# A hybrid mLSTM and Fourier mixing layer on one core: head loop rotated by four projections, value tiles finished one by one, shorter Newton chain

## The reference

```python
proj = h @ p['w_in'][l]
q, k, v, o, gt, uf, ga, gb = jnp.split(proj, SPLITS, axis=-1)
# per head and direction
s = jnp.einsum('bhtd,bhsd->bhts', qc, kc) * w
num = jnp.einsum('bhts,bhsv->bhtv', s, vc) + inter[..., None] * jnp.einsum('bhvd,bhtd->bhtv', C, qc)
den = s.sum(-1) + inter * jnp.einsum('bhd,bhtd->bht', n, qc)
h = num / jnp.maximum(jnp.abs(den), jnp.exp(-mt))[..., None]
...
hn = (hf - mu) * lax.rsqrt(var + LN_EPS) * p['mh_gain'][l].reshape(N_HEADS, DV)
y_a = (hn * og).reshape(B, S, DM).astype(h.dtype) @ p['w_branch_a'][l]
merged = jax.nn.sigmoid(ga) * y_a + jax.nn.sigmoid(gb) * y_b
return merged @ p['w_out'][l], finals
```

## Time and profile before

| | us |
|---|---|
| runs, median of 3 (lowest, highest) | 1640.36 (1639.74, 1650.82) |
| profiled execution, its own time | 1646.21 |
| its span, first to last instruction | 1644.4 |
| TensorE busy | 1518.4 (92%) |
| VectorE busy | 652.5 (40%) |
| ScalarE busy | 314.3 (19%) |
| GpSimd busy | 801.4 (49%) |

### The profile page before, as it was taken

How to read it: one execution, slowest core, us unless ns; L and a number is a source line. 1 busy time by engine, 2 the same in 40 slices (tenths; PEclk the granted TensorE clock), 3 DMA queues, 4 the chain that set the end, 5 groups by cost and what they waited for, 6 DMA issues and landing times.

```text
span 1644.4 us, 24556 instructions
## 1 busy us (share of the span) xinstructions
PE 1518.4 (92%) x9889; PEld 1476.9 (90%) x9889; DVE 652.5 (40%) x1028; ACT 314.3 (19%) x489; POOL 801.4 (49%) x365
## 2 busy tenths in 40 slices
PE   7999899999999899899886998894999999999994
PEld 7997899988989789889886998894999999999994
DVE  6422600226526525624766496457334111100114
ACT  0422211222212122122231000125211111100002
POOL 2541355652453263254147564456666666655662
PEclk9999999999999999899997999896999999999997
DMA  8220122321321221131164453310433222242221
GB/s 339 87 65 26 53 96 87 118 77 55 110 77 62 92 89 56 55 120 52 46 205 161 144 179 125 121 55 23 153 115 115 68 72 77 77 150 72 79 70 64
DMA packets 56092, 159.73 MB, mean 97 GB/s; under 512 B 5944, under 2 KB 20544, under 8 KB 54856
## 3 DMA queue, kind: packets, MB, share of 16 engines
q1 hardware_dynamic: 39464, 145.73, 25.8%
q10 hardware_dynamic: 16544, 12.82, 2.4%
HBM read 141.20 MB, written 17.33 MB: 96 GB/s over the span
## 4 chain that ended last, share of the span: by engine, by line
PE 75%; DVE 12%; issue 4%; ACT 3%; DMA 2%; POOL 2%; SPq 1%; ACTq 0%; DVEq 0%; POOLq 0%
PE psum L684 58%; PE psum L954 7%; PE psum L927 2%; PE psum L769 2%; PE psum L710 1%; PE psum L883 1%; DVE mod_sum L1419 1%; DMA mod_first<-in_wmod 1%; POOL w_hi L592 1%; PE psum L744 1%; PE psum L1015 1%; DMA raw<-in_wunits 1%; POOL r_all L656 1%; DVE h_sb L1557 1%; PE psum L843 1%
## 5 line engine op out<-in xcount | busy, mean ns | idle before, releaser
L592 POOL TENSOR_TENSOR w_hi<-raw,zero 128x1024 fp32r<-128x1024 f32 x156 | 307.1, 1969 | 652.2 <-PE psum L684 560.1
L596 POOL TENSOR_TENSOR w_lo<-raw,w_hi 128x1024 fp32r<-128x1024 f32 x164 | 413.9, 2524 | 83.2 <-ACT w_hi L1122 71.0
L684 PE MATMUL psum<-h_hi,w_hi 128*128 128x256 f32 x1600 | 373.8, 315 | 49.5 <-POOL w_lo L596 21.7
L684 PE MATMUL psum<-h_lo,w_hi 128*128 128x256 f32 x1600 | 370.9, 313 | 0.0
L684 PE MATMUL psum<-h_hi,w_lo 128*128 128x256 f32 x1600 | 369.9, 313 | 0.0
L684 PEld LDWEIGHTS psum<-h_hi,w_hi 128*128 128x128 f32 x1600 | 296.4, 193 | 53.6 <-issue 28.7
L684 PEld LDWEIGHTS psum<-h_lo,w_hi 128*128 128x128 f32 x1600 | 298.5, 192 | 0.0
L684 PEld LDWEIGHTS psum<-h_hi,w_lo 128*128 128x128 f32 x1600 | 297.4, 192 | 0.0
L1799 DVE TENSOR_TENSOR ff_sb<-psum,s_sb 128x640 f32<-128x640 f32 x22 | 18.1, 825 | 162.3 <-PE psum L684 148.8
L684 PE MATMUL psum<-f_hi,w_hi 128*128 128x256 f32 x352 | 81.4, 313 | 0.0
L684 PE MATMUL psum<-f_lo,w_hi 128*128 128x256 f32 x352 | 80.7, 311 | 0.0
(11 more groups left out here) (273 smaller groups left out, 2525.5 us busy)
## 6 DMA issues: line engine op xcount, KB each, us to landing
raw<-in_wunits SPq DMA_DIRECT2D x164, 512.0 KB, 3.5
mod_ring<-in_wmod SPq DMA_DIRECT2D x24, 512.0 KB, 4.2
mod_first<-in_wmod SPq DMA_DIRECT2D x16, 512.0 KB, 12.3
yg_dram<-yg_sb ACTq DMA_DIRECT2D x20, 256.0 KB, 2.6
yg_st<-yg_dram SPq DMA_DIRECT2D x16, 320.0 KB, 5.2
c_raw<-in_stateC SPq DMA_DIRECT2D x4, 1028.0 KB, 5.8
mod_late<-in_wmod SPq DMA_DIRECT2D x8, 512.0 KB, 4.4
raw<-in_wunits SPq DMA_DIRECT2D x8, 384.0 KB, 3.0
```

Of the source, the lines that this page charges most:

```text
L592: pool.tensor_tensor(hi, src, zero[:, 0:1].broadcast_to([P, src.shape[1]]), ALU.add)\
L596: pool.tensor_tensor(lo, src, hi.bitcast(F32), ALU.subtract).then_inc(w_split, 1)
L684: ins = mm(out[:, a:z], w[:, slot, cols], x[:, k, a:z], start=(start and n == 0), stop=(stop and n == 2))
```

## The change

- **TensorE.** Projections 0 to 3 of head 0 stand ahead of the loop, which now runs over all four heads. In it projection 0 of the next head stands between `numer(3)` and `turn(2)`, ahead of `numer(4)`; projection 1 behind `numer(4)`, projection 2 between `turn(3)` and `turn(4)`, projection 3 inside `final_states`, ahead of state 3. In the last head these four are gate units 0 to 3.
- **The values' last unit** goes tile by tile and counts up `v_done` at the end of each of the first four tiles; ScalarE waits tile by tile.
- **ScalarE and VectorE** have their parts of the next head's projections (`follow`, `qk_rest`) between their steps for tiles 2 to 4 and the states; the copy of state 3 and its store stand behind those of the fourth projection. The last head is written out, with gate units 0 to 3 in those places. Behind it ScalarE takes gate unit 4+q and then makes the `yg_hi` of group q.
- **The Newton chain** starts from half the variance and from a negative first value; each of its three rounds has two instructions in place of three. `COMBINE` goes from 15 to 12.
- SyncE and GpSimd are not touched.

```diff
@@ TensorE @@
+            def project(h, pair, tile, unit, slot):
+
+                pe.wait_ge(taken[pair], A_HEAD + (HA, HB)[pair] * h + tile + 1)
+                unit_cols(joined(pair), U_HEAD + HU * h + unit, slot, h_hi, h_lo)
@@ final_states @@
                 state(2, 6)
-                pe.wait_ge(st_act, 3 * h + 1)
+                pe.wait_ge(st_act, 3 * h + 2)
                 state(KV, 4)
+                project(h + 1, 1, 1, 3, 1)
                 pe.wait_ge(yg_ok, 5 * h + 6)
                 state(3, 7)
@@ head @@
-                project(0, 0, 0, 0)
-                if tail:
-                    turn(h - 1, 3)
-                    scores_read(h - 1)
-                project(1, 0, 1, 1)
-                if tail:
-                    turn(h - 1, 4)
-                    final_states(h - 1)
-                project(0, 1, 2, 0)
-                project(1, 1, 3, 1)
-
                 pe.wait_ge(taken[0], T[0] + 3)
                 pe.wait_ge(em_ok, 1)
-                if tail:
-                    pe.wait_ge(st_act, 3 * h)
-                    pe.wait_ge(st_dve, 2 * h)
+                pe.wait_ge(st_act, 3 * h + 1)
+                pe.wait_ge(st_dve, 2 * h + 1)
...
+                    steps = [(kk, tt) for kk in range(2) for tt in range(TT)] if q < 3 else \
+                        [(kk, tt) for tt in range(TT) for kk in range(2)]
...
+                        if k == KD - 1 and tt < TT - 1:
+                            ins.then_inc(v_done, 1)
...
                 numer(3)
+
+                project(h + 1, 0, 0, 0, 0)
                 turn(h, 2)
                 numer(4)
-
-            head(0, False)
-            with pe.Fori(1, H) as h:
-                head(h, True)
...
+                scores_read(h)
+                project(h + 1, 1, 0, 1, 1)
+                turn(h, 3)
+                project(h + 1, 0, 1, 2, 0)
+                turn(h, 4)
+                final_states(h)
+
+            project(0, 0, 0, 0, 0)
+            project(0, 1, 0, 1, 1)
+            project(0, 0, 1, 2, 0)
+            project(0, 1, 1, 3, 1)
+            with pe.Fori(0, H) as h:
+                head(h)
...
+            for j in range(4, KD):
+                pe.wait_ge(taken[j % 2], A_GA + j // 2 + 1)
+                unit_cols(joined(j % 2), U_GA + j, j % 2, h_hi, h_lo)
@@ ScalarE, head @@
-                act.wait_ge(units_done, U + 8)
                 for tt in range(TT):
+                    if tt < TT - 1:
+                        act.wait_ge(v_done, (TT - 1) * h + tt + 1)
+                    else:
+                        act.wait_ge(units_done, U + 8)
                     A_(v_hi[:, tt, 0:DV], psum[:, (0, 4, 5, 6, 7)[tt], :], ACT.Copy).then_inc(v_hi_ok, 1)
...
                 forward(h, 3)
+
+                def follow(n):
+
+                    if last:
+                        gate_a(n)
+                    else:
+                        qk(h + 1, n, k_hi if n >= 2 else q_hi, QSCALE if n >= 2 else 1.0)
+
+                follow(0)
                 turned(h, 2)
...
+                forward(h, 4)
+                follow(1)
+                turned(h, 3)
+                follow(2)
+                final_states(h)
+                turned(h, 4)
+                odd_state(h, 1)
+                follow(3)
+                odd_state(h, 3)
...
-            with act.Fori(0, H * KV // 8) as i:
-                for p in range(2):
-                    gate_a(2 * i + 2 + p, p)
-                    for r in range(4):
-                        t = 8 * i + (4 * p + r)
-                        act.wait_ge(ygs_in[r], 32 * i + 16 * (p + 1))
-                        A_(yg_hi[:, t, :], yg_st[:, r, :], ACT.Copy,
-                           scale=gain_h[:, bass.ds(t, 1)]).then_inc(ygs_hi_ok, 1)
-            for p in range(2):
-                gate_a(KD - 2 + p, p)
...
+            for q in range(H * KV // 4):
+                gate_a(4 + q)
+                for r in range(4):
+                    t = 4 * q + r
+                    act.wait_ge(ygs_in[r], 16 * q + 16)
+                    A_(yg_hi[:, t, :], yg_st[:, r, :], ACT.Copy, scale=gain_h[:, t:t + 1]).then_inc(ygs_hi_ok, 1)
@@ VectorE @@
-                    chain(v.tensor_scalar(nt_a[:], nt_a[:], -0.5, 1.5, ALU.mult, ALU.add))
-                    chain(v.tensor_tensor(nt_y[:], nt_y[:], nt_a[:], ALU.mult))
+                    chain(v.scalar_tensor_tensor(out=nt_y[:], in0=nt_a[:], scalar=1.5, in1=nt_y[:],
+                                                 op0=ALU.subtract, op1=ALU.mult))
...
                 combine(h, 3, chain)
+                if not last:
+                    qk_rest(h + 1, 0)
                 gated(h, 2)
...
+                combine(h, 4, chain)
+                if not last:
+                    qk_rest(h + 1, 1)
+                gated(h, 3)
+                if not last:
+                    qk_rest(h + 1, 2)
+                gated(h, 4)
+                odd_state(h, 1, 5)
+                if not last:
+                    qk_rest(h + 1, 3)
+                odd_state(h, 3, 7)
```

## The result

| | before | after |
|---|---|---|
| median of runs, us | 1644.29 (4 runs, 1639.74 to 1650.82) | 1672.15 (4 runs, 1667.49 to 1673.43) |
| ratio to before | | 1.0161, 95% interval 1.0133 to 1.0190 |
| span of the profiled execution, us | 1644.4 | 1669.5 |
| TensorE busy, us | 1518.4 | 1509.4 |

The change makes the kernel slower by 1.6%. TensorE is busy for 9 us less and the span is 25.1 us longer. Further runs of the kernel before moved its median from 1640.36 us to 1644.3 us beside the changed kernel and to 1643.0 to 1646.8 us beside the experiments.

A forecast was written before the change was run, and what follows sets the result against it. TensorE, busy nearly throughout, bounds the kernel; behind the head loop a chain of waits does. The loop gives 28.0 us (34.3 - 5.7 - 0.6), lost again behind it with 24 us more: 1664 us, range 1647 to 1680 us.

The forecast's parts named there:

- (a): Head loop, value tiles finished one by one: TensorE's four waits for `v_lo` go, 5.9 us less.
- (b): Head loop, next head's first projection ahead of `numer(4)`: the four long waits for `h_sb` go, 14.4 us less.
- (c): Head loop, slow clock behind the long waits, in `numer(4)` and the units after it, goes: 10.0 us less.
- (d): Head loop, gap with no releaser behind `numer(4)` at the loop's jump goes: 2.0 us less.
- (e): Second head, TensorE's waits for `yg_sb` go: 2.0 us less.
- (f): Passages between heads: value phase newly waits for the copy of state 3, about 1.9 us three times, 5.7 us more.
- (g): Head loop: `turn(4)` may wait for `gated(3)`, 0.6 us more in all, bound 3 us.
- (h): Head loop: shorter Newton chain saves 0.4 us a tile but lies beneath the inserted unit, worth nothing.
- The ring: Behind the loop: weights of unit 5+q wait for group q's `yg_lo`, `yg_hi` and gate 4+q; three rounds of 25.3 us.
- Full clock in gate units 4 to 7: Rival, behind the loop: these units take 7.04 us each despite idle times, 9.4 us less, 1655 us; chance 0.13.
- Short transfers: Rival, behind the loop: 512 KB loads land in 3.5 us, not 5.3 us, 7.2 us less, 1657 us; chance 0.12.
- The new wait dropping the clock: Rival, value phase: the wait for the copy costs 2.5 us more each time, +34 us, 1674 us; chance 0.15.

The follow-up runs named there:

- e3_state3_first: The changed kernel with the last final state, its copy and store put back ahead of the fourth projection; 1669.32 us, 1.0155 to the kernel before.
- e8_best: The changed kernel with the old `yg_hi` order, weights of gate units 4 and 5 loaded ahead, last final state ahead of the fourth projection; 1614.54 us.
- e10_unrolled: The changed kernel with old `yg_hi` order, weights loaded ahead, state 3 first, and TensorE's head loop written out; 1605.99 us, 0.9753 to the kernel before.
- e1_yg_order: The changed kernel with only ScalarE's order of `yg_hi` and gates behind the loop put back as before; 1626.17 us, 0.9907 to the kernel before.
- e9_sp_before: The kernel before with only the weights of gate units 4 and 5 loaded ahead of the wait for the states, later groups two units on; 1637.36 us.

## Why the prediction was right

The measured 1672.15 us lies in the range and is slower, as was forecast, 8 us above the forecast itself. The shift of before's own median between the two measurements (1640.4 to 1644.3 us) is half of that; the profiled span grew by 25.1 us where +24 us was forecast.

- **(a) to (e), the loop.** State 3 of the last head is done at 819.5 us, forecast 819.2 us; with two units more ahead of it that is a gain of 27.7 us against 28.0 us. All 34.3 us of (a) to (e) came: no wait for `v_lo`, four short waits for `h_sb` of 2.3 us in all as said, `numer(4)` at 1.44 us, units at 7.04 us, no gap behind `numer(4)`.
- **(f), the new wait.** Three of 1.8 us, 5.5 us, and 0.6 us of gaps without a releaser; forecast 5.7 us. No slow clock came of it. That the jump lies beneath this wait was said in (d) as an aside; the runs showed that it matters more than that: without the wait the jump costs as much (7.6 and 8.5 us of gaps in e3_state3_first and e8_best). So the size of (f) came out right, but the copy is not the only thing that sets it.
- **(g) and (h), small terms, mis-sized together.** `turn(4)` does not wait at all, where I booked 0.6 us, and the Newton chain, booked at nothing because it lies beneath the inserted unit, is what keeps it so: with the old chain it waits 2.7 us. So the inserted unit alone does not cover the old chain.
- **Behind the loop.** Unit 4 began at 836.0 us (forecast 836.5), the mix at 920.9 us (921.8); before it began at 898.9 us, half a microsecond later than the prediction read it. The ring's three rounds took 25.3, 25.2 and 25.9 us (25.3). The sum is right, two of its terms are not, and cancel: the weights took 5.9, 6.4 and 6.3 us against 5.3 us, and the unit with its hand-over to ScalarE about 9.2 us (9.3, 8.7 and 9.6) against 9.86 us. The second mix unit waited 0.2 us for its `yg_lo`, against 1 us, but TensorE then waited 1.4 us for the modulation sums, a wait that the prediction has not.
- **The rivals.** Full clock in gate units 4 to 7: they took 8.6 to 9.6 us, with a granted clock of 0.74 to 0.83 over each unit, so it did not come; but each unit reaches full clock part of the way: in the timeline the pairs of matmuls take 0.73 us for 3 to 5 us and 0.46 us from there on. Short transfers: the reverse came, 5.9 to 6.4 us behind four loads of 320 KB each. The Trainium skill's fit (DMA: Bandwidth & Descriptors, section Anatomy of one DMA), made for transfers that GpSimd issues, gives an estimate of 3.2 us, about half of what these loads of SyncE took. The new wait dropping the clock: not seen.
- **The ring as cause.** It was argued from the lists before; now it is shown from both sides: taken out of the changed kernel it gives 46 us back, put alone into the kernel before it costs 36 us in the trace.

The whole account, as it is now: the loop -27.7 us; the last state's two units of cover +14.1 us; the ring with its slow units +36 us (101.4 us from state 3 to the mix, where it was 65.8 us); and 3 us behind the start of the mix, 2 of them up to the first modulation matmuls. It makes +25 us.

## What to carry to other kernels

When a step moves in a hand-ordered schedule, follow its effect past the place it was moved for: here two gates that were moved forward put gate 4+q, in place of gate 2+q, ahead of the `yg_hi` of group q on ScalarE. The weights of that gate unit are loaded only behind the group's own tiles, and the queues closed to a ring of 25 us a round, though each engine's list looked harmless. Ask of every wait on a queue that loads weights whether the engine it feeds can still be waiting for something behind it; loads that depend on nothing belong ahead of such a wait. The version with the loads ahead, the old order, state 3 first and TensorE's loop written out runs in 1605.99 us, 2.5% below the kernel before and 66 us below the changed one.

## What the runs showed of the hardware

- A jump of TensorE's loop costs up to 2.7 us with nothing to cover it, and up to 0.8 us more a few matmuls later (2.31 and 0.76 us at the first jump of e3_state3_first, 2.67 us at its second); written out (e10_unrolled) there is no gap. Beneath a wait of 1.8 us for another engine only 0.2 to 0.3 us of it showed in the changed kernel.
- A `w_hi` on GpSimd (1.89 us alone) that becomes ready while VectorE runs `yg_lo` and modulation sums back to back ends some 1.75 us after VectorE's next gap begins, and a gap of 0.15 us is enough. In before that gap began at 877.07 us and the step took 11.43 us; in e1_yg_order (857.85 us) it took 2.52 us, in e8_best (856.03 us) 5.67 us, in e10_unrolled (854.09 us) 13.64 us. The `w_lo` right behind it, with VectorE running again, took 3.2 to 3.3 us in all four, where it takes 2.41 us alone. The same work, in another phase, is 11 us apart.
- The last store of 256 KB landed after 2.16 us by itself (the changed kernel), after 2.88 us behind ScalarE's other stores (e3_state3_first), and after 5.21 us with a load of weights beside these (e9_sp_before). That the company is the cause was not tested alone.
